# A bias table built on 8 partitions instead of 128, two early loads issued sooner, and four weight corrections in another order

## The reference, cut to what matters

```python
x = first_block(...)    # modulation, rotary retention + convolution, 16-expert choice FFN
x = second_block(...)   # SSM scan and gated linear recurrence, merged; conv FFN of width 3072
return third_block(x, ...)   # gated linear attention + sliding window, then block attention; final norm
```

```python
up = jnp.pad(gate_c * u_in, ...)
y = up[:, :, :-2] * w[0] + up[:, :, 1:-1] * w[1] + up[:, :, 2:] * w[2] + bias
out = gate_b * y
```

```python
bias = rel_bias[t5_bucket(dist)]      # rel_bias is 32 x 8
```

## Time and profile before

| | |
|---|---|
| median of 3 runs | 1962.62 us |
| the profiled execution, device time | 1962.91 us |
| its span, first to last instruction | 1961.1 us |
| PE busy | 1520.7 us (78%) |
| DVE busy | 712.4 us (36%) |
| ACT busy | 598.4 us (31%) |
| mean granted TensorE clock | 0.883 of full |
| moved by DMA | 570.24 MB, mean 291 GB/s |

### The profile page before, as it was taken

How to read it: one execution, slowest core, us unless ns; L and a number is a source line. 1 busy time by engine, 2 the same in 40 slices (tenths; PEclk the granted TensorE clock), 3 DMA queues, 4 the chain that set the end, 5 groups by cost and what they waited for, 6 DMA issues and landing times.

```text
span 1961.1 us, 24549 instructions
## 1 busy us (share of the span) xinstructions
PE 1520.7 (78%) x10333; PEld 1026.8 (52%) x10333; DVE 712.4 (36%) x1129; ACT 598.4 (31%) x1008; POOL 5.3 (0%) x8
## 2 busy tenths in 40 slices
PE   5999785655665656665556668999989999898997
PEld 3887631111211111111111128999988999797897
DVE  4457500000000000000000018768767884568564
ACT  5434410000000000000000025775755664455453
POOL 0000100000000000000000000000000000000000
PEclk8999798788787787887887888999998999899899
DMA  9555679999999999999999993433453454343230
GB/s 400 212 232 223 258 311 429 428 428 429 429 428 428 428 429 428 429 430 428 428 428 429 427 427 144 172 123 136 161 213 129 176 201 164 137 172 118 92 124 22
DMA packets 48606, 570.24 MB, mean 291 GB/s; under 512 B 4624, under 2 KB 10896, under 8 KB 12048
## 3 DMA queue, kind: packets, MB, share of 16 engines
q1 hardware_dynamic: 43072, 559.96, 69.7%
q10 hardware_dynamic: 5456, 9.15, 1.4%
HBM read 564.89 MB, written 4.19 MB: 290 GB/s over the span
## 4 chain that ended last, share of the span: by engine, by line
PE 50%; DMA 40%; DVE 6%; ACT 3%; issue 1%; SPq 0%; ACTq 0%; DVEq 0%
PE bank L1442 49%; DMA ring<-in_w_down 13%; DMA ring<-in_w_up 13%; DMA ring<-in_w_gate 13%; DMA ring<-in_w_ada 1%; ACT work L1787 1%; ACT weights_high_rounded L1787 1%; DVE rstd L2006 1%; DVE h_normed L2010 1%; DVE ring_rounded L2057 1%; DVE h_normed_rounded L2000 0%; DVE work L1281 0%; DVE small L1275 0%; DVE small L1261 0%; DVE work L1268 0%
## 5 line engine op out<-in xcount | busy, mean ns | idle before, releaser
L1442 PE MATMUL bank<-ring,work 128*32 128x512 f32 x3008 | 485.8, 779 | 310.5 <-DMA ring<-in_w_up 126.3
L1787 ACT ACTIVATE work<-bank 128x256 f32<-128x256 f32 (+3 forms) x243 | 110.5, 467 | 1107.9 <-PE bank L1442 782.6
L1442 PEld LDWEIGHTS bank<-ring,work 128*32 128x32 f32 x3008 | 93.6, 127 | 669.9 <-DMA ring<-in_w_up 206.9
L2057 DVE TENSOR_TENSOR ring_rounded<-ring,weights_high_rounded 128x1024 fp32r<-128x1024 f32 x208 | 252.8, 1222 | 136.6 <-ACT weights_high_rounded L1787 136.3
L1787 ACT ACTIVATE weights_high_rounded<-ring 128x1024 fp32r<-128x1024 f32 x244 | 255.3, 1051 | 25.9 <-PE bank L1442 25.8
L2263 DVE TENSOR_TENSOR work<-work,bank 128x512 f32<-128x512 f32 x16 | 16.5, 1029 | 592.1 <-PE bank L1442 592.1
L1442 PE MATMUL bank<-h_high_rounded,weights_high_rounded 128*128 128x256 f32 x1296 | 205.0, 297 | 18.2 <-ACT h_high_rounded L1787 16.7
L1442 PEld LDWEIGHTS bank<-h_high_rounded,weights_high_rounded 128*128 128x128 f32 x1296 | 174.8, 195 | 36.0 <-issue 23.6
L1442 PE MATMUL bank<-h_high_rounded,ring_rounded 128*128 128x256 f32 x1296 | 181.5, 282 | 6.3 <-DVE ring_rounded L2057 3.9
L1442 PE MATMUL bank<-h_normed_rounded,weights_high_rounded 128*128 128x256 f32 x1296 | 181.3, 284 | 0.0
L1442 PEld LDWEIGHTS bank<-h_high_rounded,ring_rounded 128*128 128x128 f32 x1296 | 165.8, 193 | 7.2 <-DVE ring_rounded L2057 4.3
(11 more groups left out here) (231 smaller groups left out, 1141.1 us busy)
## 6 DMA issues: line engine op xcount, KB each, us to landing
ring<-in_w_down SPq DMA_DIRECT2D x64, 2048.0 KB, 16.2
ring<-in_w_gate SPq DMA_DIRECT2D x63, 2048.0 KB, 16.1
ring<-in_w_up SPq DMA_DIRECT2D x61, 2048.0 KB, 16.4
ring<-in_dense SPq DMA_DIRECT2D x60, 2048.0 KB, 8.2
ring<-in_w_ada SPq DMA_DIRECT2D x12, 2048.0 KB, 12.7
work<-in_w_up SPq DMA_DIRECT2D x3, 1024.0 KB, 14.2
bias_diagonals<-work SPq DMA_DIRECT2D x2, 1536.0 KB, 9.5
ring<-in_dense SPq DMA_DIRECT2D x2, 1024.0 KB, 17.2
```

The lines of the kernel that those rows point to most:

```text
L1442: return nc.tensor.matmul(o, lhsT, rhs, start=start, stop=stop)
L1787: return nc.scalar.activation(o, i, f, **kw)
L2057: v.tensor_tensor(as_r(w), w, w_high[:, buffer, :], ALU.subtract).then_inc(s.w_low, 1)
```

## The change

It has three parts.

1. The bias table is made on 8 partitions. `REL_COPIES` and its copy go; PE takes `rel` itself, 33 rows by 8 columns, as the weights. `TW` is filled on partitions 0 to 7. SP writes each of the 16 lines by a DMA of its own, whose source is one row of one partition repeated 128 times. The waits on `toep_stored` count 16 DMAs instead of 2.
2. The loads of the early constants and of the decay ramps are issued right behind the two roots of the first norms, ahead of `ada_copy(0)` and of the first four high weights, and in the other order.
3. DVE's corrections of units 16, 25 and 26 move: 16 from ahead of the fourth rotation to behind it, 25 from ahead of the second reciprocal to behind both convolutions, 26 from between the convolutions to between the first two gates.

```diff
-        REL_COPIES = tiles(71, 1)[:, 0:P]
...
-                    pe.wait_ge(s.toep_sb, 1)
                     for kind in range(2):
-                        mm(B[4 + kind][:, 0:TOEP], REL_COPIES[0:REL_BUCKETS + 1, :],
+                        mm(B[4 + kind][0:AH, 0:TOEP], par("rel")[0:REL_BUCKETS + 1, :],
...
-                    fn(REL_COPIES.rearrange("p (h c) -> p h c", h=AH), spread(par("rel"), 2, P // AH),
-                       ACT.Copy).then_inc(s.toep_sb, 1)
...
-                    fn(TW[:, :, TOEP:TPITCH], ones[:, 0:2].unsqueeze(2), ACT.Copy).then_inc(s.toep_sb, 1)
+                    fn(TW[0:AH, :, TOEP:TPITCH], ones[0:AH, 0:2].unsqueeze(2), ACT.Copy).then_inc(s.toep_sb, 1)
                     for kind in range(2):
                         act.wait_ge(s.toep_mm, kind + 1)
-                        fn(TW[:, kind, 0:TOEP], B[4 + kind][:, 0:TOEP], ACT.Copy).then_inc(s.toep_sb, 1)
+                        fn(TW[0:AH, kind, 0:TOEP], B[4 + kind][0:AH, 0:TOEP], ACT.Copy).then_inc(s.toep_sb, 1)
...
-            act.wait_ge(s.toep_stored, 32)
+            act.wait_ge(s.toep_stored, 32 * AH)
...
-            sp.wait_ge(s.toep_sb, 4)
+            sp.wait_ge(s.toep_sb, 3)
             for kind in range(2):
-                copies = d["toep"][kind * AH:(kind + 1) * AH].rearrange("h (c i) j -> (h c) i j", i=AH)
-                sp.dma_start(copies, spread(TW[:, kind, :], 1, AH)).then_inc(s.toep_stored, 16)
+                for h in range(AH):
+                    sp.dma_start(d["toep"][kind * AH + h:kind * AH + h + 1],
+                                 spread(TW[h:h + 1, kind, :], 1, P)).then_inc(s.toep_stored, 16)
...
             root(1)
+            act.dma_start(consts[:, SHARED_COLS:SHARED_COLS + EARLY_COLS], d["consts"][:, SHARED_COLS:]).then_inc(s.start_in, 16)
+            act.dma_start(STARTERS, d["starters"][:, BUCKET_COLS:START_COLS]).then_inc(s.start_in, 16)
...
-            act.dma_start(STARTERS, d["starters"][:, BUCKET_COLS:START_COLS]).then_inc(s.start_in, 16)
-            act.dma_start(consts[:, SHARED_COLS:SHARED_COLS + EARLY_COLS], d["consts"][:, SHARED_COLS:]).then_inc(s.start_in, 16)
...
             for i in range(4):
-                if i == 3:
-                    lows1(16, 17)
...
-            lows1(17, 18)
+            lows1(16, 18)
...
             v.reciprocal(tiles(52, 2), tiles(52, 2))
-            lows1(24, 26)
+            lows1(24, 25)
             v.reciprocal(tiles(54, 2), tiles(54, 2)).then_inc(s.yvar_ready, 1)
             convolution(2)
-            lows1(26, 27)
             convolution(3)
+            lows1(25, 26)
             dve.wait_ge(s.yrstd_ready, 1)
             link(v.tensor_tensor(YC, YC, R4, ALU.mult))
             for i in range(3):
                 convolution_gate(i)
-                if i:
-                    lows1(26 + i, 27 + i)
+                lows1(26 + i, 27 + i)
```

## The result

The changed kernel takes 2044.08 us, the median of four runs (2043.19 to 2046.54); the kernel before took 1960.51 us beside it (four runs, 1958.0 to 1962.91). The ratio is 1.0429, with a 95% interval of 1.0409 to 1.0448: slower by 83.6 us, where 90.5 us were forecast (2053 us). The profiled execution of the changed kernel took 2042.85 us, with a span of 2041.1 us, 80.0 more than the span before. PE was busy for 1520.9 us, against 1520.7 before: no work was added, only waiting.

A forecast was written before the change was run, and what follows sets the result against it. Bounds: DMA at the start, PE from 38 to 180 us and around the table, with DMA slack there. Terms 85.1 + 1.4 + 0.9 + 1.4 + 1.7 = 90.5 us on 1962.9 gave 2053 us, range 2025 to 2085.

The forecast's parts named there:

- The bias table: Table DMAs ahead of unit 80's weight block: ACT stands 87.4 us, 2.3 us come back, +85.1 us.
- for all 16 DMAs in turn, because they go through one queue in order: Table transfer: 3.146 MB at 26.8 GB/s, one sixteenth of the best sustained rate, takes 117.5 us.
- two groups at once: Rival at the table: DMAs of different heads overlap through two openings, table takes 58.8 us, 1995 us total; chance 0.06.
- SP's issue of 14 more DMAs: SP at the table: 0.67 us each, at most 9 us, far inside the transfer time.
- The rival of one engine at 21.7 GB/s: One-partition DMAs go to a single DMA engine: table 145 us, 2080 us total; chance counted inside the forecast's 0.80.
- The early loads: At the start: 1.245 MB issued sooner share full DMA engines and delay the fourth modulation block, +1.4 us.
- inside the end of 2.9: Upper end for the early loads, 2.9 us, meant to include what a later first dense block could cost.
- Unit 16: Correction behind the fourth rotation ends at 124.02, so PE starts the low products late: +0.9 us.
- Units 25 and 26 with the clock: PE waits 4.27 us at unit 25, waits of 0.44 and 1.89 go: +1.4; half clock behind it: +1.7 us.
- That nothing is made up before the experts: Losses before the experts stay, since the experts' first blocks are issued as PE frees the ring.
- no funnel: Rival at the table: it leaves at nearly 347 GB/s, slack hides it, 5.4 us remain, 1968 us; chance 0.10.
- Not slower: Rival: no funnel and DVE corrects unit 25 in time, so 0.44 and 1.89 us are gained, 1960.6 us; chance 0.04.

The follow-up runs named there:

- two DMAs from 8: Kernel before with only the table changed: on partitions 0 to 7, written by two DMAs each reading all 8 partitions; 1990.97 us, ratio 1.014.
- sixteen spaced: Kernel before with the table on 128 partitions written by sixteen DMAs, each reading 16 partitions spaced by 8; 1968.37 us, one run.
- POOL's queue: Kernel before with only the table changed, its 16 one-partition DMAs issued by POOL instead of SP; 1989.77 us, ratio 1.0131.
- the one with the table spread out: Kernel before with only the table changed, its 16 one-partition DMAs placed between the loads of blocks 20 to 29; 1961.78 us, ratio 1.000.

## Why the prediction held, step by step

**The bias table, +85.1 forecast, +72.5 in the profile and +75.5 in the run alone.** The mechanism is as forecast: about 27 GB/s while one partition is read; the block with unit 80 late; ACT, then PE, standing. The step that was mis-sized is the transfer, "for all 16 DMAs in turn, because they go through one queue in order". The slow stretch lasted from 1433.3 to about 1535.6, 102.3 us (3.146 MB at 30.7 GB/s), not 117.5. Of the 15.2 us less, 2 are the rate (7.2 us for each DMA, not 7.34) and 13 are overlap. Between the heads of the two groups of four the windows show 43, 46 and 54 GB/s, for instance 54 from 1510 to 1515, and SP is let go sooner there, 4.62 us at 1513.35. So the rival of two groups at once was in part true: DMAs of one queue overlap where they read from different openings, here at the three switches between heads 0 to 3 and 4 to 7. The reason that the prediction gave for 26.8 GB/s, one way of sixteen for all eight partitions together, was wrong, since read together they gave 52 GB/s. The figure held because nearly all the time only one opening was in use. Against that, the block landed 9.3 us behind the end of the table, not 6.3; the two blocks behind it were issued within 12 us of it and shared the engines: from 1535.6 to 1544.9 the engines moved 399 GB/s, 3.7 MB, where the block alone has 2.1. 15.2 less and 3.0 more make the 12.2 us between 87.4 and 75.15. What came back was 2.8 us (1551.91 - 1544.88 = 7.03 for 9.84), where 2.3 was forecast. "SP's issue of 14 more DMAs", put at 9 us at most, was wrong: SP was held for 93.17 us. It did not change the sum, because the block was still issued 10 us before the table ended.

The rival of one engine at 21.7 GB/s falls with the windows: 27 GB/s, and a share of 0.86 of all 16 engines. The Trainium skill, "SBUF — State Buffer", section "Door 1: The DMA port swizzle", puts partitions 0 to 3 and 4 to 7 on two different ports. The 27 GB/s of one head, the 52 of all eight partitions and the rise at the switches agree.

**The early loads, +1.4 forecast, +2.4 by 120 us.** PE's start moved by 1.63, near the term. What was left "inside the end of 2.9" is the rest: the first dense block was pushed back as well and ACT waited 1.55 us for its second half, so PE began its dense work 3.2 us late; 0.8 came back, as more of that group ran at the fast clock (9.07 us, 9.88 before).

**Unit 16, +0.9 forecast, +1.07 measured.** Its low group began 0.94 us later, and took 1.21 us for 1.07.

**Units 25 and 26 with the clock, +3.1 forecast, +2.93 measured.** The wait was 4.04 us (4.27 forecast), the two smaller waits went, and the clock was at half from 178 to 181.

The prediction said that the waits of 0.44 and 1.89 us did nothing to the clock. That is true of the execution that it read, and not of the program. In four of the six experiments that leave this part alone (the table alone, two DMAs from 8, sixteen spaced, POOL's queue) the same wait of 1.9 us is followed by a clock of 0.52 to 0.58 from 179 to 182 us, and the stretch from there to the column sums takes 36.3 to 38.2 us for 35.0. The same window of the kernel before, then of the run with two DMAs from 8:

```profile
179.00:182.00 3.00, 2.48 (x20) 0.71 (x18) 2.48 (x5) 2.09 (x4) 0.00 (x0) 1.00 0.61 186
```

```profile
179.00:182.00 3.00, 2.70 (x13) 0.50 (x5) 2.71 (x5) 0.96 (x3) 0.00 (x0) 0.58 0.91 350
```

So the half clock that came behind the wait of 4.04 us comes in some executions of the program of before as well. On average the corrections may then cost less than in this pair. The +3.0 us of their own run fits that, but its interval is too wide to show it.

**Not foreseen: +1.65 us between 185 and 241, and it is not shown to come from the change.** The same groups of matmuls met more of the slow clock: the column sums took 6.19 us for 5.52, and the router's group 7.01 for 6.04, at a clock of 0.50 where it was 0.73 before. Windows of the changed kernel and of before:

```profile
230.00:235.00 5.00, 4.71 (x22) 4.71 (x23) 3.22 (x9) 4.51 (x10) 0.00 (x0) 0.50 1.01 424
```

```profile
222.00:227.00 5.00, 3.80 (x23) 3.80 (x23) 4.10 (x11) 4.36 (x10) 0.00 (x0) 0.73 1.00 423
```

The run without the table shows 7.01 us too. But so do three experiments in which nothing is changed up to there. PE's timeline of the run with two DMAs from 8, then of the one with the table spread out, the same program up to this point:

```profile
223.77 7.01 PE L1438 MATMUL bank<-params,h_normed 128*128 128x16 f32 x32 [3.41 <-ACT h_normed L1783]
```

```profile
223.16 6.00 PE L1450 MATMUL bank<-params,h_normed 128*128 128x16 f32 x32 [3.41 <-ACT h_normed L1795]
```

Together the small parts made 8.06 us in this pair, not 5.4. By many runs they are 4.5 to 8.6 us (the loads and corrections together), and 5.4 lies within that.

**That nothing is made up before the experts** held in this pair: the 8.06 us are the same 1180 us later. To two digits that is luck. From the experts' start to the table's copies eight of the twelve profiled executions take 1168.2 to 1168.5 us, but the run with two DMAs from 8, unchanged there, took 1164.3 and the run with loads and corrections 1164.6: its 10.3 us at 241 were 6.75 at the table.

**The total.** The table was put 12.6 us too high and the small parts 2.7 too low, so the profile's difference is 80.5 us for 90.5. The runs say 83.6; the 3 us between lie within the spread of single executions. The forecast was nearer than its largest term because two errors had opposite signs.

Of the rivals, no funnel and the single engine are out, and two groups at once was right about the partitions and wrong about the order, except at the switches. "Not slower" is out with the wait of 4.04 us; its 1960.6 us had also left out the forecast's own +1.4 and +0.9, with which it is 1962.9, no change.

## What to carry to other kernels

A DMA that repeats one row of SBUF saves on-chip copies and pays in its reading rate: count how many groups of partitions it reads, not its bytes. Before placing it, look at what stands behind it in the same queue and when that is needed; cut into pieces and placed between loads with slack, the same slow transfer is free, while another queue still left 26 of the 75 us. In a stretch where PE is bound and DVE is shared, a late correction costs PE its wait: 0.9 us late, it cost that alone; 4 us late, it was followed by some 3 us at half the clock. And compare parts of 1 or 2 us over several executions of the same program, not in one pair of profiles.

## What the runs showed of the hardware

- While one partition is read, sixteen DMA engines show a busy share of 0.83 to 0.90 at 26 to 28 GB/s. The share tells occupation, not movement.
- A queue held by slow DMAs holds its issuing engine: SP's first two issues took 0.6 us each, the third 4.45 us, and most later ones 7.18 us, as long as a transfer. With POOL as issuer the sixteen issues took 8.36 us in all, and each landed 56.2 us after its issue in the median.
- The Trainium skill, "DMA: Bandwidth & Descriptors", section "Issuing engines are not separate DMA queues", says that DMAs of all issuers run on the same 16 engines, and that several issuers save only the issue time, usually small. The shared engines agree (115 GB/s, share 1.03). The size of the saving does not: SP's issues of the table took 93.17 us, and ACT's wait was 44 us shorter with POOL as issuer.
